# A 24-row token tile of a float32-split projection: high parts and rests of x side by side in one stationary matrix

## The reference, cut to what matters

```python
h = rms_norm(x, norm_g_l)                       # x: 1024 channels a token
z = jnp.einsum('btd,dn->btn', h, w_in_l)
q, k, v, ga, qi, wi, ki, ub, gb, cv, cg, gc = split_columns(z)
```

## Time and profile before

| | us |
|---|---|
| median of 3 runs | 813.92 (811.03 to 813.96) |
| the profiled execution | 810.3 |
| its span | 809.0 |
| TensorE busy in it | 725.1 (90%) |
| VectorE busy | 558.3 (69%) |
| ScalarE busy | 323.5 (40%) |
| GpSimd busy | 292.1 (36%) |

### The profile page before, as it was taken

One profiled execution on the slowest core, in us unless ns is written; L12 is line 12 of the kernel. 1 busy time (PEld: TensorE's weight loads), 2 busy tenths in 40 slices (PEclk: granted clock), 3 DMA queues, 4 the chain that ended last, 5 costly groups with the idle time before them and its releaser, 6 DMA issues. The chain is left out here.

```text
span 809.0 us, 12852 instructions
## 1 busy us (share of the span) xinstructions
PE 725.1 (90%) x4476; PEld 592.3 (73%) x4476; DVE 558.3 (69%) x1358; ACT 323.5 (40%) x830; POOL 292.1 (36%) x320
## 2 busy tenths in 40 slices
PE   4899999997789798999998999999788779899998
PEld 3896656587668676777998865657677677777888
DVE  3538895799997986434535889679999798732322
ACT  3716455433754242234131554542383523222202
POOL 0012878712744620011120468783174565000000
PEclk9999999998898999999999999999898898999999
DMA  5543040322242546014024304030414255401202
GB/s 180 160 114 109 17 143 1 106 68 93 56 122 80 160 140 208 2 53 146 1 84 131 126 4 143 15 105 31 131 56 100 63 157 183 157 0 39 93 27 107
DMA packets 57281, 75.08 MB, mean 93 GB/s; under 512 B 13233, under 2 KB 32889, under 8 KB 57185
## 3 DMA queue, kind: packets, MB, share of 16 engines
q1 hardware_dynamic: 57106, 74.18, 30.2%
q10 hardware_dynamic: 111, 0.08, 0.0%
HBM read 67.27 MB, written 7.61 MB: 93 GB/s over the span
## 5 line engine op out<-in xcount | busy, mean ns | idle before, releaser
L1186 PE MATMUL R<-x_hi,W_r 128*128 128x268 f32 x448 | 142.8, 319 | 11.5 <-DVE bufA L1510 4.6
L1188 PE MATMUL R<-x_hi,W_r 128*128 128x268 f32 x448 | 137.3, 306 | 0.0
L1187 PE MATMUL R<-x_lo,W_r 128*128 128x268 f32 x448 | 137.3, 306 | 0.0
L1199 PE MATMUL R<-yT,W 128*128 128x268 f32 (+2 forms) x768 | 127.1, 323 | 3.7 <-DVE yT L1510 3.7
L1170 PE MATMUL R<-W_r,x_hi 128*128 128x512 f32 (+3 forms) x320 | 123.0, 384 | 6.5 <-DVE W_r L1510 6.4
L1199 PEld LDWEIGHTS R<-yT,W 128*128 128x128 f32 x768 | 109.2, 194 | 19.9 <-issue 6.7
L1171 PE MATMUL R<-W_r,x_hi 128*128 128x512 f32 (+3 forms) x320 | 119.0, 372 | 0.0
L1172 PE MATMUL R<-W_r,x_lo 128*128 128x512 f32 (+3 forms) x320 | 118.7, 371 | 0.0
L1186 PEld LDWEIGHTS R<-x_hi,W_r 128*128 128x128 f32 x448 | 94.2, 210 | 23.0 <-issue 12.4
L786 POOL TENSOR_TENSOR W_r<-W,W_r 128x1024 fp32r<-128x1024 f32 x28 | 66.7, 2391 | 94.2 <-ACT W_r L904 94.1
L1187 PEld LDWEIGHTS R<-x_lo,W_r 128*128 128x128 f32 x448 | 94.2, 210 | 0.5 <-issue 0.5
(11 more groups left out here) (243 smaller groups left out, 1275.8 us busy)
## 6 DMA issues: line engine op xcount, KB each, us to landing
W<-in_w_in SPq DMA_DIRECT2D x52, 512.0 KB, 4.7
KV<-in_cache_k SPq DMA_DIRECT2D x32, 256.0 KB, 2.8
W<-in_w_out SPq DMA_DIRECT2D x8, 1024.0 KB, 7.6
KV<-in_cache_v SPq DMA_DIRECT2D x32, 256.0 KB, 4.2
ubx<-qkv_rows SPq DMA_DIRECT2D x16, 256.0 KB, 3.5
zi<-z_rows SPq DMA_DIRECT2D x16, 196.0 KB, 3.8
W<-in_w_in SPq DMA_DIRECT2D x8, 296.0 KB, 3.4
out_new_k_prompt<-kz SPq DMA_DIRECT2D x8, 256.0 KB, 2.2
```

The source lines that it names most:

```text
L1186: pe.matmul(out, hi[:, cols], x_hi[:, kc, toks], start=(kc == 0), stop=False)
L1187: pe.matmul(out, hi[:, cols], x_lo[:, kc, toks], start=False, stop=False)
L1188: m = pe.matmul(out, lo[:, cols], x_hi[:, kc, toks], start=False, stop=(kc == KC - 1))
L1199: m = pe.matmul(R[:, k, 0:hi - lo], W[:, slot(x), kc % 4, 128 * (u[1] % 4):128 * (u[1] % 4) + 128], yT[:, kc, lo:hi], start=(kc == 0), sto ...
```

## The change

The stationary matrix of tile 0 becomes 64 columns wide: `x_few` holds 32 columns of high parts (24 of them tile 0's, 8 of its neighbour's) and beside them 32 columns of rests. Each chunk then takes two products: both halves by the high weights into partitions 0 to 63 of the bank, and the high half by the weights' rest into partitions 0 to 31. A unit of tile 0 is 16 products. Its result lies in two row blocks (0 to 23 and 32 to 55), which have to be added: the ScalarE copies the second block to `few`, the VectorE adds the first to it (`few_add`) into `few_sum`, and the ScalarE takes the unit out from there. This happens for idx, k, q and v in both layers, eight times in all. Two casts make `x_few` in each layer. The second `half_tanh` moves ahead of the first `idx_evac`, and one tap moves from behind k's tile 0 to q's tile 3.

```diff
-TAPS_IDX, TAPS_K, TAPS_Q = 8, (3, 3, 3, 3, 3), (2, 2, 2, 1, 1)
+TAPS_IDX, TAPS_K, TAPS_Q = 8, (2, 3, 3, 3, 3), (2, 2, 2, 2, 1)
...
+        x_few = sb("x_few", 128, KC, 64, dt=F32R)
+        few, few_sum = own[0:ROWS_P[0], 0, :], own[0:ROWS_P[0], 1, :]
...  scalar_layer
+            def evac_source(u):
+                n = GROUPS[G[u[0]]][2]
+                wait_unit(act, u)
+                if u[1]:
+                    return R[0:ROWS_P[u[1]], bank(u), 0:n]
+                if u[0] != "idx":
+                    wait_evac(act, (FEW[FEW.index(u[0]) - 1], 0, 0))
+                fewk_s.did(copy(few[:, 0:n], R[32:32 + ROWS_P[0], bank(u), 0:n]))
+                act.wait_ge(*fews_s.at(1 + FEW.index(u[0])))
+                return few_sum[:, 0:n]
...  the copies of idx_evac, kq_evac and of v read evac_source(u) in place of R
             half_tanh(0)
+            half_tanh(1)
             for i in range(NT):
                 idx_evac(i)
-                if i == 0:
-                    half_tanh(1)
...  tensor_layer, unit_tm
+                    if i == 0:
+                        if kc:
+                            pe.matmul(R[0:32, k, 0:n], x_few[:, kc, 0:32], lo, start=False, stop=False)
+                        m = pe.matmul(R[0:64, k, 0:n], x_few[:, kc, :], hi, start=(kc == 0), stop=(kc == KC - 1))
+                        if not kc:
+                            pe.matmul(R[0:32, k, 0:n], x_few[:, kc, 0:32], lo, start=False, stop=False)
...  before the idx units
+            pe.wait_ge(*xf_s.at(2))
...  vector_layer, behind rest(2) to rest(5)
+            if l:
+                dve.wait_ge(*xd_s.at(0))
+            else:
+                dve.wait_ge(*pre_kept.at(4))
+            xf_s.did(dve.tensor_copy(x_few[:, :, 0:32], x_hi[:, :, 0:32].bitcast(F32)))
+            xf_s.did(dve.tensor_copy(x_few[:, :, 32:64], x_lo[:, :, 0:32].bitcast(F32)))
+            def few_add(name):
+                u, n = (name, 0, 0), GROUPS[G[name]][2]
+                dve.wait_ge(*fewk_s.at(1 + FEW.index(name)))
+                fews_s.did(dve.tensor_tensor(few_sum[:, 0:n], R[0:ROWS_P[0], bank(u), 0:n], few[:, 0:n], ALU.add))
...  behind tap(1)
+                if j == 1:
+                    few_add("idx")
...  behind the taps of tile 0, ahead of kq_sum, for k and in the same way for q
+                if i == 0:
+                    few_add("k")
...
             rest(18)
             rest(19)
+            few_add("v")
```

More of the change, by code:

```diff
@@ L534, in program @@
         gt_s, ixp_s, ixr_s, ys_s = stage("gate_tanh"), stage("idxb_product"), stage("idxb_dots"), stage("sample_gated")
+        xf_s, fewk_s, fews_s = stage("few_rows_of_x"), stage("few_kept"), stage("few_summed")
+        FEW = ("idx", "k", "q", "v")
         lnd_s, lth_s = stage("ln_diag"), stage("swish_tanh")
@@ L925, in scalar_layer @@
             act.wait_ge(*rinv_s.at(1))
-            def idx_evac(i):
[L928 to L932, removed]
+            def evac_source(u):
[8 more added lines that the diff above has]
+                return few_sum[:, 0:n]
+            def idx_evac(i):
+                r, src = ROWS_P[i], evac_source(("idx", i, 0))
+                copy(zi[0:r, i, 0:256], src[:, 0:256], rinv[0:r, i:i + 1])
+                copy(zi[0:r, i, 256:288], src[:, 264:296], rinv[0:r, i:i + 1])
+                evA.did(copy(zi[0:r, i, 384:392], src[:, 256:264], rinv[0:r, i:i + 1]))
             act.wait_ge(*row_t.at(1))
@@ L965, in kq_evac @@
                 u, r = (("k", "q")[w], i, 0), ROWS_P[i]
-                wait_unit(act, u)
+                src = evac_source(u)
                 if n >= 3:
@@ L975, in kq_evac @@
                     act.wait_ge(*row_q.at(16))
-                copy(kz[0:r, n % 3, :], R[0:r, bank(u), :], rinv[0:r, i:i + 1])
+                copy(kz[0:r, n % 3, :], src, rinv[0:r, i:i + 1])
                 if n >= 2:
                     act.wait_ge(*kss_s.at(n - 1))
-                evA.did(act.activation(ksq[0:r, n % 2, :], R[0:r, bank(u), :], ACT.Square, scale=rinv[0:r, i:i + 1]))
+                evA.did(act.activation(ksq[0:r, n % 2, :], src, ACT.Square, scale=rinv[0:r, i:i + 1]))
             def kq_keep(n):
@@ L1021, in scalar_layer @@
             for i in range(NT):
-                wait_unit(act, ("v", i, 0))
-                evA.did(copy(V[0:ROWS_P[i], i, :], R[0:ROWS_P[i], bank(("v", i, 0)), :], rinv[0:ROWS_P[i], i:i + 1]))
+                evA.did(copy(V[0:ROWS_P[i], i, :], evac_source(("v", i, 0)), rinv[0:ROWS_P[i], i:i + 1]))
                 if i < 2:
@@ L1168, in unit_tm @@
                 for kc, hi, lo, more in chunks(g):
[L1169 to L1172, removed]
+                    if i == 0:
[5 more added lines that the diff above has]
+                    else:
+                        out = R[0:ROWS_P[i], k, 0:n]
+                        pe.matmul(out, x_hi[:, kc, rows], hi, start=(kc == 0), stop=False)
+                        pe.matmul(out, x_hi[:, kc, rows], lo, start=False, stop=False)
+                        m = pe.matmul(out, x_lo[:, kc, rows], hi, start=False, stop=(kc == KC - 1))
                     if more and u == LAST_UNIT[g]:
@@ L1687, in vector_layer @@
                         j += 1
+                if i == 0:
+                    few_add("q")
                 kq_sum(NT + i)
```

1 line of the change is left out of this document (added).

## The result

The changed kernel takes 824.89 us, the median of 4 runs (824.31 to 827.02). The kernel before took 812.47 us in the same comparison (4 runs, 810.17 to 813.96). The ratio is 1.0162, with a 95% interval of 1.0130 to 1.0195, so the change makes the kernel slower. The profiled execution took 824.3 us with a span of 823.0, against 810.3 and 809.0 before: 14.0 us more span.

The account below looks back on a forecast made before the run. TensorE and VectorE were both taken as full in k, and VectorE as the bound behind v. A layer's 4.1 less 0.8 gave +3.3 us, two layers +6.6, so 813.92 became 820.5 us; range 814.5 to 827.

Parts of the forecast that it names:

- The likeliest case: Whole kernel: VectorE starts the top-k rounds 3.3 us later a layer, +6.6 us in all, 820.5 us; chance 56%.
- the rival in which the clock falls in k: TensorE's 4.1 us idle in k lowers its clock, 3.4 us more in two layers, 823.9 us; chance 22%.
- Casts: Two casts for x_few ahead of VectorE's first bufA lie on the path and cost 0.42 us.
- idx: idx tile 0: -1.07 for products, +0.42 for casts, +0.7 for tile 2's wait, +0.05 us in sum, nothing won.
- Products: 8 fewer a unit, 0.134 or 0.23 us each, 13.2 us of TensorE time over two layers.
- k: k tile 0: high(12) starts 2.2 us later behind the sum, TensorE waits 4.1 us for pieces instead of 1.18.
- k's clock: Rival at k: the clock falls around TensorE's 4.1 us wait, 1.7 us of full clock lost a layer; chance 22%.
- q: q tile 0: 0.7 us won by fewer products, 0.1 lost to the sum, net +1.6 at q's end with k's 2.2.
- v: v tile 0: VectorE leaves for the attention stage 4.1 us later, 2.5 of them from waiting and summing there.
- what comes back: Behind v's sum, two VectorE products of 248 elements run beside less GpSimd work: 0.8 us returned, bounds 0 and 1.1.
- Absorbed: Rival at v: scores do not wait for the top-k rounds, only TensorE's +1.1 us a layer counts, 816.1 us; chance 15%.

Follow-up runs that it names:

- no_sum: The changed kernel without the copies and sums, tile 0 taken out of its first row block alone, so rests of x are missing: 811.04 us, ratio 1.0006.
- fill_k: The changed kernel with 16 unread products put into TensorE's wait ahead of the seventh dots in k: 821.63 us, ratio 1.0128.
- v_late: The changed kernel with v's sum alone moved, behind the second pair of top-k rounds: 824.95 us, ratio 1.0162.
- v_old: The changed kernel with v's tile 0 alone as it was before the change: 821.44 us, ratio 1.0141.
- casts_late: The changed kernel with the two casts alone moved, from ahead of VectorE's first bufA to behind rest(7): 822.10 us, ratio 1.0153.
- k_high: The changed kernel with high(12) alone moved between k's copy and k's wait for the sum: 820.07 us, ratio 1.0118.
- mended: The changed kernel with high(12) between k's copy and wait, v's sum and the casts later, idx's sum ahead of tap(0): 813.66 us, ratio 1.0036.
- k_old: The changed kernel with k's tile 0 alone as before, 24 products, no copy, no sum: 821.08 us, ratio 1.0115.

## Why the prediction was right, and where it was not

The forecast said slower, and the range held the time. The likeliest case did not win: its sum was +6.6 us, the rival in which the clock falls in k had +10.0, and the runs show +12.4 between medians and +14.0 between profiled executions. That 824.9 us lies so near that rival's 823.9 is partly luck, since its price was too low and falls that it did not name added to it. The steps:

- **Casts:** 0.42 us forecast; their starts and that of bufA (37.16, 37.36, 37.56) give 0.40.
- **idx:** nothing won was forecast, and from the first bufA to the first turned tile of idx the changed kernel needs 0.06 us more in layer 0 than the kernel before, so that nothing was won. The wait of the third tile was forecast at 0.7 and is 0.69.
- **Products:** 0.13 and 0.23 us each, no price for 64 columns: right. That they would be saved but stand in waits was right too, and the waits of no_sum show it. I had said that TensorE's busy time would fall by some 10 us; it fell by 2.8, because I left the clock out of that number.
- **k:** the seventh dots were forecast at 87.7 behind a wait of 4.1 us; they are at 87.89 behind 4.28. The chain was the one described: copy ended at 78.5, tap at 80.0, kz at 80.70, `high(12)` at 81.95 (forecast 81.85).
- **k's clock** is the step that failed. I took it as a rival at 22% and 1.7 us a layer, the smaller of the two cases in the earlier trace rows, and put nothing for it in the sum. It fell in both layers for twice as long as at 134 us, and cost 2.5 and 2.8 us. fill_k shows the cause. The nearest row was the 4.60 us wait of the earlier trace rows with 0.52 behind it; it, and not the 1.60 us wait, is close to 4.1 us in length. The reason I gave against, that k's waits so far had left the clock whole, rested on waits of 1.18 us. The Trainium skill (TensorE: Matmul & The Clock Gate, Why this matters for your kernels) advises against gaps in mid-kernel; here the trace agrees (4.28 us idle, 0.50 from 87 to 91 us).
- **q:** forecast -0.7 for the products and +0.1 for the sum. Measured are -0.16 us in both layers (+4.94 to +4.78, +13.51 to +13.35). ScalarE's copy and wait for the sum lie in the relus' way there. That this takes just the missing 0.4 us was not tested.
- **v:** forecast +2.5 for wait and sum, 0.8 back. Measured are 3.2 and 2.9 us (2.60 and 2.29 of wait, 0.6 of sum), since the last four products ran at the low clock in layer 0, 0.42 us apart (161.59, 162.00) and not 0.23, and in layer 1 the last of them; and 1.9 back. The forecast also counted a step of 0.23 us too many, as the last of four products starts three steps after the first. The products of 248 elements came 6.5 us later in layer 0 and not 4, most of it k's delay. Net +1.3 and +1.0 where I had +1.7. The bound of 1.1 for what comes back was too low. The conv products went from 1.05 to 0.36 us each, and those of `rel` and the following instruction gained as well. The Trainium skill (SBUF — State Buffer, Who interferes with whom) has two SBUF inputs contend with GpSimd's reads; the trace agrees, with 0.72 us for two behind the end of GpSimd's work and 2.09 beside it. GpSimd's last instruction on q ahead of them in the changed kernel, then its work beside them in v_late:

```profile
163.84 0.46 POOL L836 TENSOR_TENSOR kz<-rot_tmp 128x128 f32<-128x128 f32 x1
163.37 1.62 POOL L833 TENSOR_TENSOR kz<-kz,gam 128x512 f32<-128x512 f32 x1
```

- **Absorbed:** this rival has a part of the truth. From tile 1 of v on TensorE runs without a gap up to the first scores, before (548.7 to 572.3 us) and after (562.0 to 586.7). So those scores do not wait for the top-k rounds, and the 1.1 us that they lose in v is not the sum's: the clock fell there for 3.4 us (161.7 and 561.0). fill_k has the same sum and no fall, and comes 0.4 and 0.5 us sooner there. The waits between the halves of v's tile 0, longer by the products saved, go with it: behind 2.15 us the clock fell in 13 of 16 places over all traces, behind 1.23 in none of 12. VectorE's lateness shows only at the second group of scores, where TensorE waits for the top-k rounds: 1.4 and 1.1 us there, 0.9 in fill_k, 0.0 in v_old and no_sum. That wait is 4.57 us in layer 1, as long as before, and not the 6.8 that I forecast: TensorE comes later by as much as VectorE does, the one by the clock and the other by the sum.

Put together, in us: from the end of idx to the seventh dots 2.6 and 2.6, q -0.2 twice, v 1.4 and 1.1 at the second group of scores (with the fall that before had at 135 us taken out of layer 0), casts 0.4 in layer 1: 7.7, against the forecast sum of 6.6. The clock adds 2.5 and 2.8 in k, 1.6 behind the 3.12 us wait in layer 1 (438 us) and 1.0 in the stretch with 0.72 at 314 us, and gives 1.6 back at 139 us, where it no longer falls: 6.3. The two make 14.0 us. Terms of up to 0.6 us at the start, at the end and in layer 0's attention are left out; they cancel. The split of k is shown by fill_k; the pieces at 314 and 438 us are read from the trace and were not tested. casts_late, which takes the wait at 433 us back to 2.71, still has a clock of 0.72 behind it, so that the casts are the cause of the fall at 438 us is not shown. Over all traces it looks likelier with them: at this place the clock fell in 7 of 7 traces with the wait of 3.11 or 3.12 us, and in 3 of 7 with 2.71 or 2.72.

## What to carry to other kernels

Before removing work from an engine, look at what ends the wait behind it: where the next engine's work is due at a fixed time, the saving becomes a wait, and a wait in TensorE's list can cost more than its length. A partial result that two other engines must pass to and fro should not stand ahead of work that others wait for; put that work between the copy and the wait, as k_high does. When a forecast adds a wait, price the clock with the row whose wait is nearest in length, not with the mildest one, and keep a range for it: the same wait met a fall in one kernel and none in the next.

## What the runs showed of the hardware

**Waits and the clock.** I counted, in the traces, whether the granted clock was at 1.2 GHz right behind TensorE's waits in k. Behind 4.28 or 4.29 us it was in 8 of 8 (both layers of the changed kernel, v_old, v_late and casts_late), each time for 6.8 us. Behind 2.00 us it was in 4 of 4 (k_high and mended), for 3.4 or 6.8 us. Behind 1.18 us it was in none of the kernels with that wait. Behind the 2.35 us wait in q it was in 9 of 18 places, among them both layers of k_old and v_late and neither of no_sum and mended, so the length alone does not decide.

**Work that nobody reads can pay.** 15 unread products a layer, in waits of 1.18 to 1.60 us, made the kernel before 0.45% faster (0.9955 [0.9929, 0.9980]).

**Beside GpSimd.** The same two VectorE products of 248 elements took 2.09 us in v_late and 0.72 us in the changed kernel, where they started at 164.75, 0.4 us after GpSimd had ended its work on q.
